# First attention layer: the order of scores, share transposes and output products along six steps

## The reference

```python
q = (_rms_norm(x, g_norm) @ w_q).reshape(b, n_chunks, CHUNK, B_HEADS, B_HEAD_DIM)
...
sc = jnp.einsum('bqhd,bkhd->bhqk', q_c, k_c).astype(jnp.float32) * ATTN_SCALE + bias
sc = jnp.where(valid, sc, NEG_INF)
p = jax.nn.softmax(sc, axis=-1).astype(v_c.dtype)
return jnp.einsum('bhqk,bkhd->bqhd', p, v_c)
...
return o @ w_o
```

## Time and profile before

| | us |
|---|---|
| median of three runs | 1316.07 (1315.05 to 1316.51) |
| profiled execution, its own time | 1314.8 |
| its span, first to last instruction | 1313.0 |
| of that, TensorE busy | 1243.5 |
| attention steps, from the first scores to the first product of the feed-forward net | 406.9 to 487.6 |

### The profile page before, as it was taken

The page is one execution under the profiler, slowest core; times in us unless marked ns, Lnnn a source line. Parts: engine busy times, 40 slices in busy tenths (PEclk is TensorE's granted clock), DMA queues, the critical chain, the costliest instruction groups (busy, mean ns, idle before and its releaser), DMA issues.

```text
span 1313.0 us, 14873 instructions
## 1 busy us (share of the span) xinstructions
PE 1243.5 (95%) x6219; PEld 1038.9 (79%) x6219; DVE 707.8 (54%) x712; ACT 545.7 (42%) x652; POOL 65.5 (5%) x119
## 2 busy tenths in 40 slices
PE   6998999999999989999989999999988767999998
PEld 5886888888889878888878888889877656788887
DVE  4657455445555745555455445458556545545552
ACT  4534344434445434445334434336553131443341
POOL 4100000000000000100010000031000010000000
PEclk9998999999999889999999999999988885899999
DMA  7753466555484327655635655646541022366550
GB/s 272 256 192 118 138 198 202 193 192 202 160 286 154 97 65 238 221 175 182 215 128 188 192 192 197 199 146 199 177 137 35 30 81 64 96 224 192 189 196 32
DMA packets 147825, 218.46 MB, mean 166 GB/s; under 512 B 5136, under 2 KB 115760, under 8 KB 147632
## 3 DMA queue, kind: packets, MB, share of 16 engines
q1 hardware_dynamic: 144640, 206.69, 47.6%
q0 software_dynamic: 3120, 10.84, 2.4%
HBM read 216.45 MB, written 1.05 MB: 166 GB/s over the span
## 4 chain that ended last, share of the span: by engine, by line
PE 88%; DVE 6%; ACT 2%; issue 1%; DMA 1%; POOL 1%; SPq 0%; DVEq 0%; POOLq 0%; ACTq 0%
PE acc L1607 27%; PE acc L1609 26%; PE acc L1608 26%; PE turn L1593 4%; DVE w_lo L1032 1%; DVE xt L1042 1%; ACT w_hi L722 1%; DMA raw<-in_a_w_in 1%; ACT work L935 1%; PE acc L1842 1%; PE turn L1948 1%; DVE xn L1057 0%; PE turn L1822 0%; PE acc L1733 0%; PE turn L1967 0%
## 5 line engine op out<-in xcount | busy, mean ns | idle before, releaser
L1032 DVE TENSOR_TENSOR w_lo<-raw,w_hi 128x2048 fp32r<-128x2048 f32 (+1 forms) x196 | 442.4, 2279 | 202.6 <-ACT w_hi L722 202.4
L1607 PE MATMUL acc<-w_hi,xt 128*128 128x512 f32 (+2 forms) x1112 | 441.4, 397 | 23.9 <-DVE xt L1042 21.9
L1609 PE MATMUL acc<-w_hi,xt 128*128 128x512 f32 (+2 forms) x1112 | 433.5, 390 | 0.0
L1608 PE MATMUL acc<-w_lo,xt 128*128 128x512 f32 (+2 forms) x1112 | 432.9, 389 | 0.0
L722 ACT ACTIVATE w_hi<-raw 128x2048 fp32r<-128x2048 f32 (+1 forms) x196 | 368.0, 1907 | 153.6 <-PE acc L1609 124.5
L1607 PEld LDWEIGHTS acc<-w_hi,xt 128*128 128x128 f32 x1112 | 214.2, 193 | 70.3 <-DVE xt L1042 23.3
L1609 PEld LDWEIGHTS acc<-w_hi,xt 128*128 128x128 f32 x1112 | 213.5, 192 | 43.0
L1608 PEld LDWEIGHTS acc<-w_lo,xt 128*128 128x128 f32 x1112 | 214.4, 193 | 40.3
L1607 PE MATMUL acc<-w_hi,ht 128*128 128x512 f32 x352 | 139.6, 397 | 0.0
L1609 PE MATMUL acc<-w_hi,ht 128*128 128x512 f32 x352 | 138.0, 392 | 0.0
L1608 PE MATMUL acc<-w_lo,ht 128*128 128x512 f32 x352 | 136.6, 388 | 0.0
(11 more groups left out here) (247 smaller groups left out, 904.9 us busy)
## 6 DMA issues: line engine op xcount, KB each, us to landing
raw<-in_ffn_w_gate_up SPq DMA_DIRECT2D x88, 512.0 KB, 5.1
raw<-in_ffn_w_down SPq DMA_DIRECT2D x22, 1024.0 KB, 5.0
raw<-in_ffn_wg SPq DMA_DIRECT2D x44, 512.0 KB, 4.1
raw<-in_ffn_wu SPq DMA_DIRECT2D x44, 512.0 KB, 5.1
raw<-in_ffn_wd SPq DMA_DIRECT2D x22, 1024.0 KB, 5.1
raw<-in_a_w_in SPq DMA_DIRECT2D x16, 1024.0 KB, 6.2
raw<-in_w_in SPq DMA_DIRECT2D x10, 1024.0 KB, 5.4
raw<-in_a_w_out SPq DMA_DIRECT2D x8, 1024.0 KB, 5.2
```

The costliest lines, as they stand in the source:

```text
L1032: V.tensor_tensor(w_lo[:, u % RING, 0:kt * w], raw[:, u % RAW, 0:kt * w], w_hi[:, u % RING, 0:kt * w].bitcast(F32), ALU.subtract).then_inc ...
L1607: mm(o, lhs[0], rhs[0], start=start, stop=False)
L1608: mm(o, lhs[0], rhs[1], start=False, stop=False)
L1609: return mm(o, lhs[1], rhs[0], start=False, stop=stop)
```

## The change

Only the order of the attention's six steps changes, and with it the numbers of the `turn` banks. No instruction is added to or taken from what the engines compute.

- On TensorE `scores(i + 1)` now stands ahead of `turn_shares(i)` in every step. Of the output pieces, `out_tile(0, 1, 0)` moves ahead of `scores(3)`, `out_tile(0, 0, 0)` between `turn_shares(3)` and `values(3)`, `out_tile(1, 1, 0)` between `turn_shares(4)` and `values(4)`, `out_tile(0, 0, 1)` ahead of `values(5)` and `out_tile(0, 1, 1)` behind it.
- On VectorE `shift(i + 1)` stands ahead of `shares(i)`, `heads_out(0, 0)` behind `shares(1)`, and the last of the four `U_O` splits ahead of `shift(3)`.
- On ScalarE `read_kq(5)` and `read_kq(6)` stand ahead of `exps(1)` and `exps(2)`, and `high_out(0, 0)` ahead of the split of the third `U_O` unit.

```diff
@@ -239,16 +239,11 @@
     for i in range(6):
+        if i < 5:
+            N_S1.append(banks(2))
         N_P1.append(banks(2))
-        if i == 4:
-            N_S1.append(banks(2))
-            T_O[0, 1] = splits(1)
...
+        if i in (1, 3, 4, 5):
+            T_O[{1: (0, 0), 3: (1, 0), 4: (0, 1), 5: (1, 1)}[i]] = splits(1)
@@ -855,13 +850,13 @@
             exps(0)
             read_kq(4)
             split_to(U_O + 1)
+            read_kq(5)
             exps(1)
-            read_kq(5)
             split_to(U_O + 2)
+            read_kq(6)
             exps(2)
-            read_kq(6)
+            high_out(0, 0)
             split_to(U_O + 3)
-            high_out(0, 0)
             read_kq(7)
@@ -1235,25 +1230,25 @@
             shift(0)
+            shift(1)
             shares(0)
-            shift(1)
             split_to(U_O + 1)
+            shift(2)
+            shares(1)
             heads_out(0, 0)
-            shares(1)
-            shift(2)
             split_to(U_O + 2)
             low_out(0, 0)
             split_to(U_O + 3)
+            split_to(U_O + 4)
+            shift(3)
             shares(2)
-            shift(3)
+            shift(4)
             heads_out(1, 0)
-            split_to(U_O + 4)
             shares(3)
-            shift(4)
             low_out(1, 0)
+            shift(5)
             heads_out(0, 1)
             shares(4)
-            shift(5)
             low_out(0, 1)
             shares(5)
             residual(2, C_O, U_O + 3, 0)
@@ -1870,39 +1865,41 @@
             scores(0)
             kq_tile(4, 1)
             kq_tile(5, 0)
+            scores(1)
             turn_shares(0)
-            scores(1)
             kq_tile(5, 1)
             values(0)
             kq_tile(6, 0)
+            scores(2)
             turn_shares(1)
-            scores(2)
             kq_tile(6, 1)
+            turn_heads_out(0, 0, 1)
             values(1)
-            turn_heads_out(0, 0, 1)
             kq_tile(7, 0)
             kq_tile(7, 1)
+            pe.wait_ge(*freed(T_O[0, 0][0]))
+            pe.wait_ge(s_kq, 7)
+            out_tile(0, C_O % 2, 0)
+            scores(3)
             turn_shares(2)
-            pe.wait_ge(*freed(T_O[0, 0][0]))
-            pe.wait_ge(s_kq, 8)
-            out_tile(0, 0, 0)
-            scores(3)
             values(2)
-            out_tile(0, 1, 0)
+            scores(4)
             turn_shares(3)
-            scores(4)
+            out_tile(0, 1 - C_O % 2, 0)
+            values(3)
             turn_heads_out(1, 0, 2)
-            values(3)
+            scores(5)
             turn_shares(4)
-            scores(5)
+            pe.wait_ge(*freed(T_O[1, 0][0]))
+            pe.wait_ge(s_o, 3)
+            out_tile(1, C_O % 2, 0)
+            values(4)
             turn_heads_out(0, 1, 3)
-            values(4)
+            turn_shares(5)
             pe.wait_ge(*freed(T_O[0, 1][0]))
             out_tile(0, 0, 1)
+            values(5)
             out_tile(0, 1, 1).then_inc(s_half, 1)
-            turn_shares(5)
-            out_tile(1, C_O % 2, 0)
-            values(5)
             pe.wait_ge(s_o, 4)
             out_tile(1, 1 - C_O % 2, 0)
             turn_heads_out(1, 1, 4)
```

## The result

The changed kernel takes 1322.01 us (median of ten, 1319.29 to 1327.40) against 1315.58 us (median of ten, 1314.58 to 1317.57): ratio 1.0057, 95% interval 1.0038 to 1.0075. It is slower, by 0.57%. The forecast was +6.2 us, 1322.3; measured are +6.4. What the median does not show is the spread: 8 us between the fastest and the slowest run, against 3 us before.

What follows compares the result with a forecast made beforehand. TensorE, busy 1243.5 of 1313.0 us, was taken as the bound. Waits 12.6 plus low clock 5.0 give 17.6 lost against 11.4 before: +6.2 on 1316.07 makes 1322.3 us, range 1318.0 to 1327.5.

Steps and rivals of the forecast that it cites:

- The case called the likeliest: The clock falls once, at `values(2)`; +6.2 us, 1322.3 us, own range 1320.5 to 1324, chance 0.47.
- The loss to be had, 11.4 us: In the old attention stretch, TensorE loses 5.5 us to waits and 5.9 to low clock; all a new order can win.
- Steps 0 and 1: `values(0)` and `values(1)` stay covered; the turn of the first heads, ahead of `values(1)`, waits a new 1.5 us.
- Step 2: `values(2)` waits a new 3.7 us for copies behind `shift(3)`; the hoisted split accounts for under 1.
- Step 3: Ahead of `values(3)`, a wait of 1.0 us at the full clock, nothing at the low one.
- Step 4: `out_tile(1, 1, 0)` waits a new 3.3 us for `heads_out(0, 1)`, which stands behind `shift(5)`.
- The tail: `out_tile(0, 0, 1)` waits 0.5 us instead of 1.16, `heads_out(1, 1)` costs 2.2 instead of 0.85, the last turned tile's 1.41 stays.
- The clock: The wait at `values(2)` brings the clock down, 0.50 from about 446 to 457; 5.0 us extra.
- rival 2: The clock falls more than once, also at `out_tile(1, 1, 0)` or ahead of `values(1)`; 1324.3 to 1328.3 us, chance 0.30.
- The sign of being wrong that I had named: A second low-clock stretch after 465 us would show the forecast wrong; no size given.
- Rival 3: The clock holds throughout the stretch, so only waits count; +2.2 us, 1318.3 us, chance 0.10.
- Rival 4: Copies not late at `values(2)` and `out_tile(1, 1, 0)`, VectorE's `shift` running under an output piece; -4.8 us, 1311.3, chance 0.07.

Runs made afterwards that it cites:

- Experiment 4: A new order, same instructions, in which large work or already finished results cover each wait, ScalarE's list rearranged too; 1304.90 us, ratio 0.9909 to the kernel before.
- experiment 3: The changed kernel with the split of the fourth `U_O` unit put back behind `heads_out(1, 0)` on VectorE; 1323.51 us, ratio 1.0053.
- Experiment 1: The changed kernel with `turn_shares(2)` again ahead of the output piece and `scores(3)`, and `shares(2)` ahead of `shift(3)`; 1317.76 us, ratio 1.0012.
- experiment 9: The changed kernel once more, unaltered, for a second profiled execution and more times; 1325.09 us, ratio 1.0064.
- experiment 6: The changed kernel with `turn_shares` and `shares` of 2 and 4 back in the old order, `heads_out(0, 1)` ahead of `shift(5)`; 1315.98 us, ratio 0.9999.
- experiment 2: The changed kernel with twelve additional products that nothing reads between `turn_shares(2)` and `values(2)`; 1320.95 us, ratio 1.0039.
- experiment 5: The kernel before with only output pieces dealt out on TensorE, ahead of `values(3)`, `values(4)` and `values(5)`; 1311.60 us, ratio 0.9964.
- 7: The changed kernel with `heads_out(0, 0)` back ahead of `shift(2)` on VectorE and its turn behind `values(1)` on TensorE; 1323.31 us, ratio 1.0052.
- 8: The changed kernel with `values(5)` behind `out_tile(0, 1, 1)` instead of ahead of it; 1322.03 us, ratio 1.0038.
- experiment 10: Experiment 4 with `scores(3)` ahead of `turn_shares(2)`, `values(2)` directly behind it, and the split and `shift(3)` ahead of `shares(2)`; 1311.08 us, ratio 0.9965.

## Why the prediction was right

The waits and what ends them came as laid out, and the median came within 0.3 us of the forecast. The second is in part luck. The case called the likeliest, one fall of the clock, was to cost 6.2 us; the execution with one fall took 1319.29, which is 4.5 above the profiled execution of the kernel before (1314.8), and 5.5 more in the stretch. Other executions fall more often and cost more than 6.2. An overrated single fall and an underrated number of falls met near the middle.

- **The loss to be had, 11.4 us.** Right. Experiment 4 recovered 10.9 of the stretch and 11.8 of the median that its own comparison had for the kernel before (1316.71).
- **Steps 0 and 1.** Covered, as said: no wait at V(0) or V(1). The turned heads waited 1.36, forecast 1.5.
- **Step 2.** Wait 3.61, forecast 3.7, with the mechanism as given. The split's share was forecast as under 1, and experiment 3 measured 0.8. Experiment 1 shows that undoing this step brings back about four fifths of the loss in the medians.
- **Step 3.** Forecast was no wait under the low clock; 0.62 was left (0.39 in the second execution). The clock came back at about 453.4, earlier than I had it.
- **Step 4.** Wait 3.20, forecast 3.3. The release by `heads_out` was right; the profile's name for it, "issue", was not what I had said it would show.
- **The tail.** 0.54, 2.21 and 1.41, forecast 0.5, 2.2 and 1.4.
- **The waits in sum:** 1.36 + 3.61 + 0.62 + 3.20 + 0.54 + 2.21 + 1.41 = 12.95, forecast 12.6.
- **The clock.** This is the mis-sized term. I had one fall from about 446 to 457, 5.0 us of extra time, as the likeliest, and several falls as a rival with 0.30. The rows show 6.8 us of low clock in the fastest execution, so 3.4 us at most, and 17.0 us, so up to 8.5, in another. Of the ten runs six lie between 1319.3 and 1322.2 and four between 1326.6 and 1327.4; with experiment 9, half of sixteen lie in rival 2's range, 1324.3 to 1328.3, only four in the forecast's own, 1320.5 to 1324, and four below that. So rival 2, which had a chance of 0.30, was as common as everything else together. The sign of being wrong that I had named, a second low stretch behind 465, is absent in the fastest execution and present in experiment 9's (466 to 472 and 486 to 490). Nor does a wait between large products always leave the clock alone, as the 1.76 of the earlier trace rows suggested: the same wait stands in all twelve profiled executions, and in experiment 6 (at 679) it is followed by 3.4 us at the low clock.
- **Rival 3** (the clock holds throughout) did not occur in an execution of the changed kernel that was profiled; experiment 2's profiled execution shows it, with one of the waits filled, at 1316.78. The rival's +2.2, added to the profiled 1314.8, gives 1317.0.
- **Rival 4** (faster) needed 4.8 of 7.0 us of waits gone. They were all there. But experiment 5 shows that its idea was sound for the pieces dealt out in the old order: a piece that does not stand behind a `shift` does cover.

On the Trainium skill's charge of half of the throttled time (TensorE: Matmul & The Clock Gate, "HAM oscillation — how this bites in real kernels"): between the two executions of the changed kernel it would say 5.1 us for 10.2 us more of low clock, and 4.2 were measured. Here it was an upper bound. Part of the low time costs nothing because TensorE waits in it anyway: in experiment 9 the clock fell at 465.7, 1.1 us before the wait at step 4 ended at 466.79, and the wait ahead of V(3) shrank from 0.62 to 0.39.

The twelve profiled executions, the kernel before among them, can be laid side by side to see which wait the clock falls at. Windows of 2 us give this table; a fall is counted at a wait when it lies in it or up to 2.2 us behind its end.

| Wait | Length, us | Executions that have it | Of these, the clock fell |
|---|---|---|---|
| ahead of V(2), not filled | 2.8 to 3.6 | 6 (changed kernel, 3, 7, 8, 9, 10) | 6 |
| ahead of O(1, 1, 0) | 2.3 to 3.2 | 7 (changed kernel, 1, 2, 3, 7, 8, 9) | 5 (not changed kernel, 2) |
| ahead of O(1, 0, 0) | 2.2 | 7 (changed kernel, 1, 2, 3, 6, 7, 9) | 4 (3, 6, 7, 9) |
| ahead of the first turned heads | 1.4 | 7 (changed kernel, 1, 2, 3, 6, 8, 9) | 2 (3, 6) |

So the fall at V(2), the one that was forecast, came every time, and the others sometimes. Behind V(2) stands the most light work, `values`, `scores` and transposes in a row, as the prediction had it; no run isolates this. The length alone does not sort the waits: 2.8 us ahead of V(2) brought a fall in experiments 3 and 10, and 3.2 ahead of O(1, 1, 0) did not in two executions. The record also has the mean granted clock of each whole run: 0.962 to 0.965 for the six fast runs of the ten, 0.960 or 0.961 for the four slow ones. A mean lower by 0.001 is 2.6 us more at 1.2 GHz in 1317 us, whose half is 1.3. The fastest run has 0.965 and the slowest 0.961; by this estimate the clock accounts for some 5 of the 8 us of spread.

What stays open is what decides in a single run whether the clock falls at the last three of these waits. The table tells how often it did, in one execution of each program but the changed kernel, and not how often each program would.

## What to carry to other kernels

Running one step ahead pays only if the engine that is asked for two things does first the one that somebody waits for: a copy of 0.6 us behind a `shift` of 3 us cost the 3 us wherever no large work covered it. So put the independent pieces between the transposes and their use, or ahead of the transposes where the `shift` can run under them (V(3) in experiment 4), and look in the other engine's list at what stands ahead of the result. In this kernel a wait of 3 us between small matmuls cost about twice its length in the median (experiment 10). Look at the spread of the runs as well as at the median: where the waits are fixed and the times still spread, as in experiment 9, the clock is the first thing to look at.

## What the runs showed of the hardware

- A wait of 2.79 us put into an otherwise full stretch cost 6.2 us in the median, where the profiled execution had 3.4 us at 1.2 GHz behind it; its slowest run is 9.4 above the other kernel's median.
- With identical waits, one program had 6.8 us at 1.2 GHz in one execution and 17.0 in another, and its sixteen times spread over 8.4 us (1319.3 to 1327.7), eight of them up to 1322.2 and six from 1326.6 on.
- Twelve products of no use in a wait of 3.6 us went with a clock of 2.4 GHz through the whole stretch in the one execution that was profiled, which reached the last wait 2.5 us earlier than the one without them. All six profiled executions with such a wait left unfilled had a fall there.
